# Two small tiles moved in front of the low weight tiles, so that the low weight tiles lie 64 bytes further within 512 bytes

## The chip, the cores and the metric

The kernel runs on one core of one Trainium2 chip. The metric is the time of one execution on the device in microseconds; a version's time is the median of its runs. One further execution was profiled, and all durations below come from that one.

## What is computed

Three transformer layers over one sequence of 256 tokens with 1024 features, in float32: an mLSTM layer and a short-convolution layer, each followed by a squared-ReLU MLP of width 4096, then a layer with retention and pooling, cross-attention to a memory of 256 tokens, and a gated MLP with a convolution. Nearly all of the arithmetic is the products of the activations with dense weight matrices:

```python
for i in range(DEPTH):                       # 2 layers
    h = rms_norm(x, g[0])
    h = mlstm_mixer(h, ...) if i % 2 == 0 else short_conv_mixer(h, ...)
    x = x + rms_norm(h, g[1])
    h = sqrelu_mlp(rms_norm(x, g[2]), w_mlp_up[i], w_mlp_down[i])
    x = x + rms_norm(h, g[3])
# then one layer more
h = rmsnorm(x, mix_norm_g)
x = x + concat([y_ret, y_pool]) @ w_out      # retention and pooling, from h @ w_in
x = x + cross_attn(rmsnorm(x, xa_norm_g), mem_n, xa_wq, xa_wkv, xa_wo)
x = x + conv_glu_ffn(rmsnorm(x, ffn_norm_g), ffn_w_up, ffn_conv_w, ffn_conv_b, ffn_w_down)
return rmsnorm(x, final_norm_g)
```

## The kernel before

**Tiles.** The activations lie transposed, features on the 128 partitions and the 256 tokens along a row, as 8 chunks (`x`, [128, 8, 256]). All weights come from memory as one sequence of slabs, in the order in which they are used. A slab is 1 MB, [128, 2048] float32: 8 blocks of the contraction by 256 output columns. The loads go to four tiles `raw0` to `raw3` in turn (line 366, SyncE).

**Splitting.** A product of two float32 numbers is made of three products of shorter ones. Each slab is split in halves of 1024 columns. ScalarE writes the high part, rounded to fp32r, into `wH` (line 790), and VectorE writes what is left, `raw - wH`, into `wL` (line 1230). There are two tiles of each, `wH0`, `wH1`, `wL0`, `wL1`, used in turn. The activations are split in the same way into `xnH` (line 804, ScalarE) and `xnL` (line 1237, VectorE), the memory into `memH` and `memL` (line 1244), the mixers' outputs into `mixH` and `mixL` (line 1272), the MLPs' hidden values into `hH` and `hL`.

**Products.** For each block of 128 by 128 weights TensorE runs three matmuls with 256 moving columns, each with a weight load of its own (lines 404 to 406):

```python
pe.matmul(psum[:, n, 0:T], wH[w][:, wc], aH[:, ac, :], start=start, stop=False)
pe.matmul(psum[:, n, 0:T], wH[w][:, wc], aL[:, ac, :], start=False, stop=False)
return pe.matmul(psum[:, n, 0:T], wL[w][:, wc], aH[:, ac, :], start=False, stop=stop)
```

In the phases that want tokens on the partitions (lines 431 to 433) the activations are the stationary operand, and `wH`, `wH`, `wL` the moving one. Other small products are put between the blocks of a slab by hand (`between`): sums of squares for the norms (line 472), scores, transposes.

**Order.** Every engine has its own written order and waits on semaphores. TensorE waits for the low half of the weights (`weights_ready`), and ScalarE, before it writes `wH` again, for the slab two before. VectorE and ScalarE also take the results out of the two PSUM tiles `po`. GpSimd adds squares for the norms (lines 1793 to 1800), computes the inverse roots (line 1806) and adds part of the residual (line 1817).

**Where the tiles lie.** SBUF is laid out by hand by `sb`, which hands out addresses within a partition one after the other, each size rounded up to 32 bytes:

```python
place = [nc.sbuf_base + (-nc.sbuf_base) % 64]
def sb(name, shape, dt, at=None):
    size = int(np.prod(shape[1:])) * 4
    if at is None:
        off = place[0]
        place[0] += (size + 31) // 32 * 32
```

The base is 16512, which is 128 past a multiple of 512. Each of `raw`, `wH`, `wL` and `x` takes 8192 bytes, a multiple of 512, so in the kernel before all of them begin 128 bytes past a multiple of 512, and so does `par`, the table of gains (1312 bytes). `warm` (4 bytes, written once at the start, line 854) and `ms` (8 bytes, the mean squares of a norm, line 1250) follow, 32 bytes each. `xnH`, `xnL`, `memH`, `memL`, `memk`, `memv`, `y`, `squares`, `mem`, `hH`, `hL`, `mixH` and `mixL` begin 64 bytes past a multiple of 512; `cgate` and `cval` of the last MLP 128 past it, `apad` 64 and 96 past it.

Of the kernel before, what the change touches and what calls it, by code (L numbers as in the profile page):

```python
# [9 lines left out]
P = 128  # L10
T = 256
TT = T // P
# [60 lines left out]
def build(nc, xT, memT, pos, weights, wgate, params, poolw, tri, mask, select, decay, freq, recount, out):  # L73
    f32, f32r, i32 = mybir.dt.float32, mybir.dt.float32r, mybir.dt.int32
# [3 lines left out]
    with ctx:  # L78
# [7 lines that stand above are left out]
            else:  # L86
                off = at[0]
                at[0] += (size + 31) // 32 * 32
            return nc.alloc_sbuf_tensor_at(name, list(shape), dt, offset=off)
# [4 lines left out]

        raw = [sb(f"raw{i}", [P, SLAB], f32) for i in range(RAW)]
        wH = [sb(f"wH{i}", [P, SLAB], f32r) for i in range(HL)]
        wL = [sb(f"wL{i}", [P, SLAB], f32r) for i in range(HL)]
        x = sb("x", [P, C, T], f32)
        par = sb("par", [P, NPAR], f32)
        warm = sb("warm", [P, 1], f32)  # L100
        ms = sb("ms", [P, TT], f32)
        minus_half = sb("minus_half", [P, 2 * NH], f32)
        rtok = sb("rtok", [P, TT], f32)
        rmem = sb("rmem", [P, TT], f32)
# [1896 lines left out]
```

## Time and profile before

| | |
|---|---|
| median of 3 runs | 995.93 us (992.37 to 1000.08) |
| the profiled execution's own time | 998.9 us |
| its span, first to last instruction | 996.5 us |
| mean granted TensorE clock | 0.994 of full speed |
| TensorE matmuls busy | 960.1 us, 96% |
| VectorE busy | 660.3 us, 66% |
| ScalarE busy | 534.8 us, 54% |
| GpSimd busy | 186.4 us, 19% |
| DMA | 49.5% of the 16 engines' time, 172 MB |

The profiled execution took 2.4 us more than its span. Matmuls are pipelined: a record of one lasts longer than the distance to the next, so several are in flight, and what an engine achieves is read from how many start in a stretch of time and not from the duration of one. Idle time stands with the engine that waited, together with what released it.

### The profile page before, as it was taken

What the parts mean: (1) busy time and instruction counts of PE and PEld (TensorE: products, weight loads), DVE (VectorE), ACT (ScalarE), POOL (GpSimd) and SP (SyncE); (2) the same over time, 40 slices, a digit from 0 to 9 for tenths busy, and PEclk for the clock granted to TensorE, in tenths of its full rate; (3) what the DMA queues carried; (4) which work ended last, traced back from release to release, by engine and by line L of the source; (5) the groups of instructions that cost most, each with busy time, mean ns of one, the idle gap of its engine ahead of it and who ended that gap; (6) DMA issues with size and microseconds to landing.
All of it is one profiled execution on the core that took longest, in us unless ns stands there. A gap on an engine that the chain in (4) does not pass through costs nothing.

```text
span 996.5 us, 20181 instructions
## 1 busy us (share of the span) xinstructions
PE 960.1 (96%) x8062; PEld 946.0 (95%) x8062; DVE 660.3 (66%) x843; ACT 534.8 (54%) x754; POOL 186.4 (19%) x159
## 2 busy tenths in 40 slices
PE   8999989999999899989999999889999999999995
PEld 7999989999999799989999999889999999999995
DVE  6667586665444877678665444774775779999642
ACT  5566646654444545556655443545554566666541
POOL 2121140000000400149100010455120122222101
PEclk9999999999999999999999999999999999999998
DMA  8533635555555355535655554544443545555521
GB/s 341 191 127 120 218 127 192 191 174 206 173 197 180 112 197 199 179 129 201 211 179 201 207 174 154 205 145 164 139 158 105 178 142 179 200 181 198 210 87 43
DMA packets 25844, 172.17 MB, mean 173 GB/s; under 512 B 3252, under 2 KB 3892, under 8 KB 5432
## 3 DMA queue, kind: packets, MB, share of 16 engines
q1 hardware_dynamic: 25784, 171.30, 49.5%
q8 instruction: 46, 0.75, 0.3%
q14 instruction: 14, 0.11, 0.0%
HBM read 170.24 MB, written 1.05 MB: 172 GB/s over the span
## 4 chain that ended last, share of the span: by engine, by line
PE 63%; DVE 15%; issue 6%; POOL 2%; ACT 2%; DVEq 1%; ACTq 0%; POOLq 0%
PE po L404 19%; PE po L405 19%; PE po L406 19%; DVE wL L1230 7%; DVE xnL L1237 2%; POOL rtok L1806 2%; DVE cval L1741 1%; DVE cgate L1741 1%; DVE apad L1728 1%; ACT wH L790 1%; PE po L432 1%; PE po L433 1%; PE po L431 1%; PE pn L479 1%; PE pc L728 1%
## 5 line engine op out<-in xcount | busy, mean ns | idle before, releaser
L1230 DVE TENSOR_TENSOR wL<-raw,wH 128x1024 fp32r<-128x1024 f32 x318 | 411.7, 1318 | 157.7 <-ACT wH L790 157.3
L790 ACT ACTIVATE wH<-raw 128x1024 fp32r<-128x1024 f32 x318 | 332.3, 1057 | 255.7 <-PE po L406 226.7
L404 PE MATMUL po<-xnH,wH 128*128 128x256 f32 x1376 | 391.4, 284 | 18.9 <-DVE xnL L1237 13.4
L405 PE MATMUL po<-xnL,wH 128*128 128x256 f32 x1376 | 383.6, 279 | 0.0
L406 PE MATMUL po<-xnH,wL 128*128 128x256 f32 x1376 | 383.4, 279 | 0.0
L404 PEld LDWEIGHTS po<-xnH,wH 128*128 128x128 f32 x1376 | 259.2, 188 | 24.3 <-DVE xnL L1237 10.3
L405 PEld LDWEIGHTS po<-xnL,wH 128*128 128x128 f32 x1376 | 260.5, 189 | 0.2
L406 PEld LDWEIGHTS po<-xnH,wL 128*128 128x128 f32 x1376 | 260.0, 189 | 0.0
L404 PE MATMUL po<-hH,wH 128*128 128x256 f32 x688 | 191.4, 278 | 1.3 <-DVE wL L1230 1.3
L405 PE MATMUL po<-hL,wH 128*128 128x256 f32 x688 | 191.3, 278 | 0.0
L406 PE MATMUL po<-hH,wL 128*128 128x256 f32 x688 | 191.3, 278 | 0.0
L1793 POOL TENSOR_TENSOR squares<-squares 128x512 f32<-128x512 f32 x26 | 39.7, 1526 | 515.9 <-ACT squares L838 362.1
L404 PEld LDWEIGHTS po<-hH,wH 128*128 128x128 f32 x688 | 129.1, 188 | 1.5 <-DVE wL L1230 1.5
L405 PEld LDWEIGHTS po<-hL,wH 128*128 128x128 f32 x688 | 130.2, 189 | 0.0
L406 PEld LDWEIGHTS po<-hH,wL 128*128 128x128 f32 x688 | 129.3, 188 | 0.0
L404 PE MATMUL po<-mixH,wH 128*128 128x256 f32 x256 | 71.8, 281 | 1.0 <-DVE mixL L1272 1.0
L405 PE MATMUL po<-mixL,wH 128*128 128x256 f32 x256 | 71.0, 277 | 0.0
L406 PE MATMUL po<-mixH,wL 128*128 128x256 f32 x256 | 71.0, 277 | 0.0
L1497 DVE SCALAR_TENSOR_TENSOR hrelu<-po,Rs 128x512 f32<-128x512 f32 x32 | 22.1, 691 | 49.2 <-PE po L406 49.0
L1237 DVE SCALAR_TENSOR_TENSOR xnL<-x,par,xnH 128x256 fp32r<-128x256 f32 x56 | 48.5, 918 | 7.4 <-ACT xnH L804 7.4
L404 PEld LDWEIGHTS po<-mixH,wH 128*128 128x128 f32 x256 | 48.1, 188 | 1.5 <-DVE mixL L1272 1.4
L405 PEld LDWEIGHTS po<-mixL,wH 128*128 128x128 f32 x256 | 48.3, 189 | 0.0
(284 smaller groups left out, 1083.8 us busy)
## 6 DMA issues: line engine op xcount, KB each, us to landing
raw<-in_weights SPq DMA_DIRECT2D x158, 1024.0 KB, 4.8
x<-in_xT SPq DMA_DIRECT2D x4, 256.0 KB, 5.7
raw<-in_weights SPq DMA_DIRECT2D x2, 512.0 KB, 5.5
mem<-in_memT SPq DMA_DIRECT2D x1, 1024.0 KB, 13.1
out<-y SPq DMA_DIRECT2D x4, 256.0 KB, 2.4
decayt<-in_decay SPq DMA_DIRECT2D x1, 512.0 KB, 3.7
poolwt<-in_poolw SPq DMA_DIRECT2D x1, 256.0 KB, 3.6
par<-in_params SPq DMA_DIRECT2D x1, 164.0 KB, 3.4
```

Source lines behind the costliest of these rows:

```text
L404: pe.matmul(psum[:, n, 0:T], wH[w][:, wc], aH[:, ac, :], start=start, stop=False)
L405: pe.matmul(psum[:, n, 0:T], wH[w][:, wc], aL[:, ac, :], start=False, stop=False)
L406: return pe.matmul(psum[:, n, 0:T], wL[w][:, wc], aH[:, ac, :], start=False, stop=stop)
L431: pe.matmul(psum[:, t, 0:256], aH[:, k, tc], wH[w][:, wc], start=k == 0, stop=False)
L432: pe.matmul(psum[:, t, 0:256], aL[:, k, tc], wH[w][:, wc], start=False, stop=False)
L790: act.activation(wH[b % HL][:, hs], raw[b % RAW][:, hs], ACT.Copy).then_inc(s_hi, 1)
L1230: dve.tensor_tensor(wL[b % HL][:, hs], raw[b % RAW][:, hs], wH[b % HL][:, hs].bitcast(f32), ALU.subtract)\
L1237: k = dve.scalar_tensor_tensor(xnL[:, c, :], x[:, c, :], col(gain, c), xnH[:, c, :].bitcast(f32), ALU.mult, ALU.subtract)
L1497: dve.scalar_tensor_tensor(hrelu[n % 2][:, :, :], slot(GROUP0[up] + n)[:, :, 0:T], 0.0, over_pair(Rs[:, :]), ALU.max, ALU.mult).then_inc(s ...
L1741: k = dve.scalar_tensor_tensor(c, apad[n % 2][:, e, tap:tap + T], w, c, ALU.mult, ALU.add)
L1793: pool.tensor_tensor(sq[0], sq[0], sq[p], ALU.add).then_inc(s_sqa, 1)
L1806: pool.tensor_tensor(r[:, :], ms[:, :], minus_half[:, 0:TT], ALU.pow).then_inc(s_r, 1)
```

## The change

Two declarations move up by a few lines. No instruction, wait, loop or transfer is added, removed or put elsewhere; each engine runs the same list of instructions in the same order, with other addresses in some operands.

```diff
         raw = [sb(f"raw{i}", [P, SLAB], f32) for i in range(RAW)]
         wH = [sb(f"wH{i}", [P, SLAB], f32r) for i in range(HL)]
+        warm = sb("warm", [P, 1], f32)
+        ms = sb("ms", [P, TT], f32)
         wL = [sb(f"wL{i}", [P, SLAB], f32r) for i in range(HL)]
         x = sb("x", [P, C, T], f32)
         par = sb("par", [P, NPAR], f32)
-        warm = sb("warm", [P, 1], f32)
-        ms = sb("ms", [P, TT], f32)
         minus_half = sb("minus_half", [P, 2 * NH], f32)
```

`warm` and `ms` take 32 bytes each. `wL0`, `wL1`, `x` and `par` therefore begin 64 bytes later, 192 past a multiple of 512. `warm` and `ms` now lie between `wH1` and `wL0`. `minus_half` and everything behind it, `xnH` and `xnL` among it, stay at their addresses, and so do `raw` and `wH`.

## Rows read from the trace of the kernel before

**Rows 1.** The page: busy us of each engine, and granted clock in 40 slices.

```profile
PE 960.1 (96%) x8062; PEld 946.0 (95%) x8062; DVE 660.3 (66%) x843; ACT 534.8 (54%) x754; POOL 186.4 (19%) x159
PEclk9999999999999999999999999999999999999998
```

**Rows 2.** Who waited for whom: us in total, times, longest us.

```profile
ACT wH L790 <- PE po L406: 226.7, 176, 4.4
DVE wL L1230 <- ACT wH L790: 157.3, 102, 6.2
...
PE po L404 <- DVE xnL L1237: 13.4, 11, 2.3
...
PE po L404 <- DVE wL L1230: 4.3, 5, 2.4
```

**Rows 3.** Stretches: us, busy (instructions) of PE, PEld, DVE, ACT, POOL; clock, DMA, GB/s.

```profile
160.00:320.00 160.00, 160.00 (x1361) 160.00 (x1360) 84.68 (x85) 79.08 (x92) 3.33 (x3) 1.00 0.55 186
455.00:600.00 145.00, 145.00 (x1281) 145.00 (x1281) 86.75 (x84) 80.07 (x97) 23.26 (x21) 1.00 0.56 192
880.00:930.00 50.00, 50.00 (x426) 50.00 (x426) 48.59 (x64) 30.31 (x43) 10.41 (x9) 1.00 0.55 189
```

**Rows 4.** Two of the weight loads' groups, 160 to 320 us: count | busy, mean ns.

```profile
L405 PEld LDWEIGHTS po<-xnL,wH 128*128 128x128 f32 x200 | 38.4, 192 | 0.0
L404 PEld LDWEIGHTS po<-xnH,wH 128*128 128x128 f32 x199 | 37.3, 188 | 0.0
```

**Rows 5.** Two of the groups of weight loads, 880 to 930 us.

```profile
L406 PEld LDWEIGHTS po<-xnH,wL 128*128 128x128 f32 x119 | 22.8, 192 | 0.0
L405 PEld LDWEIGHTS po<-xnL,wH 128*128 128x128 f32 x118 | 22.1, 188 | 0.0
```

**Rows 6.** Two of the groups of weight loads, 130 to 136 us.

```profile
L404 PEld LDWEIGHTS po<-memH,wH 128*128 128x128 f32 x15 | 2.9, 192 | 0.0
L406 PEld LDWEIGHTS po<-memH,wL 128*128 128x128 f32 x15 | 2.8, 188 | 0.0
```

**Rows 7.** Tile wL: duration ns min/median/max, first and last start us.

```profile
L406 PE MATMUL po<-xnH,wL x1376: 276/276/415, 9.6 to 921.6; 128*128 128x256 f32 x197
L1230 DVE TENSOR_TENSOR wL<-raw,wH x318: 1207/1221/2370, 7.7 to 974.1; 128x1024 fp32r<-128x1024 f32 x159
L433 PE MATMUL po<-wL,xnH x96: 276/279/281, 40.3 to 686.5; 128*128 128x256 f32 x96
```

**Rows 8.** Groups of the whole span: count | busy us, mean ns | idle before.

```profile
L406 PE MATMUL po<-xnH,wL 128*128 128x256 f32 x1376 | 383.4, 279 | 0.0
L406 PE MATMUL po<-hH,wL 128*128 128x256 f32 x688 | 191.3, 278 | 0.0
L406 PE MATMUL po<-mixH,wL 128*128 128x256 f32 x256 | 71.0, 277 | 0.0
```

**Rows 9.** VectorE's groups of lines 1237, 1244, 1266 and 1272, whole span.

```profile
L1237 DVE SCALAR_TENSOR_TENSOR xnL<-x,par,xnH 128x256 fp32r<-128x256 f32 x56 | 48.5, 918 | 7.4 <-ACT xnH L804 7.4
L1244 DVE SCALAR_TENSOR_TENSOR memL<-mem,par,memH 128x256 fp32r<-128x256 f32 x8 | 3.5, 474 | 0.0
L1266 DVE TENSOR_TENSOR sigo<-po,Rs 128x512 f32<-128x512 f32 x4 | 2.7, 687 | 0.8 <-PE po L406 0.8
L1272 DVE TENSOR_TENSOR mixL<-mixf,mixH 128x512 fp32r<-128x512 f32 x4 | 2.8, 689 | 1.1 <-ACT mixH L849 1.1
```

**Rows 10.** In order of time: start us, us; VectorE and GpSimd around line 1237.

```profile
132.14 0.89 DVE L1237 SCALAR_TENSOR_TENSOR xnL<-x,par,xnH 128x256 fp32r<-128x256 f32 x2 [1.16 <-ACT xnH L804]
...
630.16 5.95 DVE L1237 SCALAR_TENSOR_TENSOR xnL<-x,par,xnH 128x256 fp32r<-128x256 f32 x6
...
631.64 1.55 POOL L1793 TENSOR_TENSOR squares<-squares 128x512 f32<-128x512 f32 x1 [0.28 <-ACT squares L807]
...
634.22 1.61 POOL L1800 TENSOR_TENSOR squares<-squares 128x256 f32<-128x256 f32 x2
```

**Rows 11.** Duration of line 1741's groups, ns min/median/max.

```profile
L1741 DVE SCALAR_TENSOR_TENSOR cval<-apad,par,cval x44: 475/480/485, 815.7 to 929.4; 128x256 f32<-128x256 f32 x44
```

## The prediction, made before the changed kernel ran

> **What bounds the kernel now.** I read the page first, then who waited for whom, then the groups, and last single stretches of TensorE. TensorE has matmuls in flight for 96% of the span, and its clock is at the upper level (2.4 GHz) in every slice but a part of the last [rows 1]. ScalarE waits 226.7 us for TensorE, and VectorE waits 157.3 us for ScalarE, so the two splitting engines stand behind TensorE most of the time and not ahead of it. TensorE waits for the low weights only 4.3 us, in 5 waits, and 13.4 us for `xnL` behind a norm [rows 2]. So the end is set by how fast matmuls follow each other. A change of addresses can act in three ways: on that distance, on the duration of VectorE's, ScalarE's and GpSimd's operations, or on the transfers. I take them in turn.
>
> **How fast the matmuls follow each other.** The reader should count them. From 160 to 320 us, 1361 touch the stretch; two of these straddle its edges, so the distance is 160 us / 1359 = 117.7 ns. From 455 to 600 us it is 145 us / 1279 = 113.4 ns. Both stretches run at full clock with no idle time and the same work (an up projection, then the down projection) [rows 3]. So TensorE has two paces, 4.3 ns apart, and it keeps one for more than a hundred microseconds. This looks just like the trace of a bank conflict, and an address change might be aimed at it. The groups of weight loads tell what it is. At the slower pace one load in three takes 192 ns and the other two 188. In 160 to 320 us that is the load of line 405, from `wH` [rows 4]. In 880 to 930 us it is that of line 406, from `wL`, while the load of `wH` at line 405 has 188 [rows 5]. In 130 to 136 us it is that of line 404, again from `wH` [rows 6]. The addresses within 512 bytes are the same in all these stretches: weights at 128, activations at 64. A conflict between fixed addresses would sit on one of the three lines. This one sits on any of them, so it is a rhythm of the weight loads and matmuls with a period of three, that starts anywhere and then holds. Matmul durations go with it. In the phases by token, where the stationary operand is at 64 and the moving one at 128, the matmuls of line 433 also range between 276 and 281 ns [rows 7]: turning the distance of the two operands round did not remove either pace.
>
> **The change part by part.** It adds, removes and moves no instruction, and each queue and each wait stays. What is left is operands.
>
> *TensorE's reads of `wL`.* 2416 of its matmuls in the rows (1376 + 688 + 256 + 96) use `wL` [rows 7, 8], one in each triple. The 8 slabs that are multiplied with the memory add 8 x 16 = 128, which makes 2544 triples. What it costs: by the argument above, 0. What it could at most gain is the whole slow pace. I size that from mean durations, 276 ns at the fast pace and 281 at the slow one, the ends of line 433's durations. Line 406 with `xnH` has 383.4 us / 1376 = 278.6 ns, so 0.53 of those are at the slow pace; with `hH` 191.3 / 688 = 278.1, so 0.41; with `mixH` 71.0 / 256 = 277.3, so 0.27 [rows 7, 8]. Over these three that is (729 + 282 + 69) / 2320 = 0.47 of the triples. The same share of all 2544 triples is 1196 triples or 3588 matmuls; 3588 x 4.3 ns = 15.4 us. The other end: the 4044 at the fast pace all turn slow, 4044 x 4.3 ns = 17.4 us more. Two ends, -15 and +17 us, and I take 0, since the rows for no link to the address are direct.
>
> *VectorE's writes of `wL` (line 1230).* Today all three operands stand at 128. The median is 1221 ns for 1024 columns [rows 7]. Line 1272, all at one place too, needs 689 ns for 512 columns, and line 1266, which has one operand in PSUM, 687 [rows 9]. So two SBUF operands at the same place cost no more than one, and (1221 - 689) / 512 = 1.04 ns is the price of each further column, and that leaves no conflict to remove in line 1230. Tiles that differ by 64 already meet in `cval<-apad,cval` (apad at 64 or 96, cval at 128), with 475 to 485 ns for 256 columns [rows 11], against 474 for line 1244 with all tiles at 64 [rows 9]: nothing to lose either. I take 0. The ends: if line 1230 ran at no more than the columns' 1.04 ns, so 1065 ns, TensorE could gain what it waits for it, 4.3 us [rows 2]. The other end is the next point.
>
> *VectorE's reads of `x` (line 1237).* This is where the groups can mislead. `xnL<-x,xnH` takes 918 ns in the mean and `memL<-mem,memH`, the same operation on the same columns, 474 [rows 9]. `x` is at 128 and `xnH` at 64, while `mem` and `memH` are both at 64. Read as the price of lying 64 bytes apart, it would be 444 ns on 256 columns, and four times that on each half slab: 318 x 1.78 us = 565 us on VectorE, which would then be busy for 1225 us and bound the kernel. In order of time the cause is another one. The two at 132.14 us run in 0.89 us together, thus some 445 ns each, with the same addresses; between 132 and 133 us GpSimd has no row. The six from 630.16 us take 5.95 us, beside additions of GpSimd, one in 1.55 and two in 1.61 us among them [rows 10]. The stall belongs to GpSimd's work, and the change leaves that as it is.
>
> The Trainium skill, "SBUF — State Buffer", section "SBUF: two separate sides", says that engines contend only at a port pair that VectorE and GpSimd share, and that the loser is blocked for the whole instruction. By that rule the 918 ns are waits for GpSimd and the sum stays at 0; by the reading of addresses it would be +229 us. The trace agrees with the rule, by the 0.89 us for two.
>
> *The rest.* ScalarE's reads of `x` and GpSimd's additions into `x` are off the path, and ScalarE waits for TensorE anyway [rows 2]. `warm` is written once and `ms` 13 times with two elements. Transfers into `x` and `par` happen at the start, and `raw` keeps its place. I take 0 for all; a microsecond either way covers them.
>
> **The sum.** 998.9 us (the profiled execution) + 0 = 998.9 us. That execution lies 3.0 us above the median of the runs, and within the 7.7 us that they spread over. The forecast for a median is therefore the median before, 995.9, rounded to 996 us. A difference under 1% (10 us) can't be told from none with runs that spread so far. The spread itself may well be the share of the slow pace from run to run: 10 us would need 2300 of 7632 matmuls to change their pace.
>
> **The rivals.**
>
> *The slow pace goes (faster).* If the third load of each triple reads from another place than the first two, the rhythm of three may find no hold. For it: it has the same period as the sequence `wH`, `wH`, `wL`. Against it: the slow load was found on all three lines. It would give 995.9 - 15.4 = 980.5; from 880 to 930 us VectorE is nearly full, 48.59 of 50 us [rows 3], and would become the bound there, which keeps some 426 x 4.3 ns = 1.8 us. So 982 us.
>
> *The slow pace takes all (slower).* The place is the weight load of line 406, each time that TensorE turns from `wH` to `wL` and back. Until now the distance between the place of the weights and that of the activations never changes within a triple; with the change it does, and if that step itself costs what the slow load costs, each triple has its slow load and no stretch finds the fast pace. Price: 4.3 ns on each of the 4044 matmuls now fast, +17.4 us, 1013 us. It passes 1% when the slow share goes from 0.47 past 0.47 + 10 / (7632 x 0.0043) = 0.77. Against it: by token the distance is turned round, and the fast pace is there all the same [rows 7].
>
> *Tiles 64 bytes apart stall VectorE (much slower).* As worked out above, 1225 us. The 445 ns speak against it.
>
> *VectorE's split gets shorter.* 996 - 4.3 us, so 992 us: within 1%, even with as much again.
>
> *The change doesn't do what it says.* The shift might not be 64. 32 + 32 bytes are reserved for `warm` and `ms`, and nothing else moves ahead of `wL`, so I give it nothing of its own; the time would be 996 as well.
>
> **How the numbers follow.** No effect: 0.74. The slow pace goes, or goes for the most part: 0.12. The slow pace takes all, or most: 0.08. A shorter split: 0.05. VectorE stalls: 0.01. The predicted time is that of the likeliest case, 996 us. Its own range is 990 to 1002, from the runs before (992.4 to 1000.1) and a little on either side for a median of few runs. The range given goes toward the two rivals of pace without holding them whole: 984 to 1005. The chances: faster by over 1% 0.13 (the rival of pace, and a little of the case with the shorter split); slower by over 1% 0.09 (the two slower rivals); within 1% 0.78.
>
> **What would show it right or wrong.** Right: the matmuls still follow at 113.4 or 117.7 ns, both paces occur, perhaps in other stretches, and a slow load can be found on line 404 or 405, whose tile didn't move. Line 1230 keeps a median of 1221 ns, line 1237 its 0.45 us where GpSimd is idle, line 1272 its 689. TensorE's waits for lines 1230 and 1237 stay at some 4 and 13 us. The share of the slow pace may differ between two executions of one kernel; then a difference in one profile says nothing of the address. Wrong: a third pace, or no slow stretch at all, or slow loads only on line 406, or a median of line 1230 or 1237 that moved by more than a few ns.

## The result, and the profile after

The changed kernel takes 1016.76 us in the median of 4 runs (1015.28 to 1017.18). The kernel before has one run more than ahead of the change, and its median over the four is 998.0 us (992.37 to 1000.76). The ratio is 1.0192, with a 95% interval from 1.0146 to 1.0238: slower by nearly 2%. The profiled execution took 1016.92 us, its span is 1014.6 us against 996.5.

The page of the changed kernel, engines and clock first [rows 1], then the groups of the splits and of the matmuls with `xnH` and `xnL` [rows 8, 9]:

```profile
span 1014.6 us, 20181 instructions
...
PE 982.4 (97%) x8062; PEld 969.4 (96%) x8062; DVE 659.8 (65%) x843; ACT 536.8 (53%) x754; POOL 187.3 (18%) x159
...
PEclk9999999999999999999999999999999999999997
...
L1230 DVE TENSOR_TENSOR wL<-raw,wH 128x1024 fp32r<-128x1024 f32 x318 | 411.3, 1317 | 165.9 <-ACT wH L790 165.5
...
L404 PE MATMUL po<-xnH,wH 128*128 128x256 f32 x1376 | 397.0, 289 | 16.7 <-DVE xnL L1237 12.4
L405 PE MATMUL po<-xnL,wH 128*128 128x256 f32 x1376 | 388.8, 283 | 0.0
L406 PE MATMUL po<-xnH,wL 128*128 128x256 f32 x1376 | 386.1, 281 | 0.0
...
L1237 DVE SCALAR_TENSOR_TENSOR xnL<-x,par,xnH 128x256 fp32r<-128x256 f32 x56 | 48.5, 918 | 7.4 <-ACT xnH L804 7.4
```

The added time lies on TensorE: 982.4 us busy where it was 960.1, with the same 8062 matmuls. The mean granted clock is 0.991, where it was 0.994, and it is 1.00 in the stretch shown below for both kernels. VectorE's busy time, ScalarE's and GpSimd's moved by 2 us at most. Line 1237 has its 918 ns unchanged, though `x` now lies 128 bytes from `xnH` and not 64.

Who waited for whom, with the lines that answer to [rows 2]:

```profile
ACT wH L790 <- PE po L406: 254.8, 196, 4.4
DVE wL L1230 <- ACT wH L790: 165.5, 107, 6.2
...
PE po L404 <- DVE xnL L1237: 12.4, 11, 2.3
...
PE po L404 <- DVE wL L1230: 1.8, 1, 1.8
```

The two engines that split the weights wait longer than before, 254.8 us for 226.7 and 165.5 for 157.3, and TensorE waits for `wL` 1.8 us for 4.3. So the slower engine is TensorE itself. The stretch from 160 to 320 us shows how (columns as in [rows 3], without the other engines). First the view by stretch of the changed kernel, then its groups of matmuls with `xnH` and `xnL`, then the same groups of the kernel before:

```profile
160.00:320.00 160.00, 160.00 (x1356) 1.00 0.55 189
```

```profile
L404 PE MATMUL po<-xnH,wH 128*128 128x256 f32 x205 | 57.9, 283 | 0.0
L405 PE MATMUL po<-xnL,wH 128*128 128x256 f32 x205 | 57.7, 282 | 0.0
L406 PE MATMUL po<-xnH,wL 128*128 128x256 f32 x205 | 57.3, 280 | 0.0
```

```profile
L406 PE MATMUL po<-xnH,wL 128*128 128x256 f32 x201 | 56.5, 281 | 0.0
L404 PE MATMUL po<-xnH,wH 128*128 128x256 f32 x200 | 56.2, 281 | 0.0
L405 PE MATMUL po<-xnL,wH 128*128 128x256 f32 x200 | 56.2, 281 | 0.0
```

Matmuls follow each other at 160 us / 1354 = 118.2 ns, neither of the two old paces. And the three lines no longer have one duration: 283, 282 and 280 ns in place of 281 for all three in this stretch before. The tile `wL` now lies at 192 within 512 bytes as the allocator gives it, so the change did what it says.

In the whole trace of after no long stretch runs at 113.4 ns. I went through the starts of all matmuls, 30 at a time, and kept the groups in which all are of lines 404 to 406 and follow each other without a gap. In after the mean distance of every one of 185 such groups lies between 118.2 and 118.5 ns. In before 106 of 180 lie at 113.3 and the other 74 at 117.8.

### The profile page after: what moved, and what is told of

It reads as the page before. It is cut to its first block, busy times and chain, and to the rows that moved or that the text cites. A ratio compares the mean times of both kernels' runs of the same rounds, so it can differ in the third digit from the quotient of the medians.

```text
span 1014.6 us, 20181 instructions
## 1 busy us (share of the span) xinstructions
PE 982.4 (97%) x8062; PEld 969.4 (96%) x8062; DVE 659.8 (65%) x843; ACT 536.8 (53%) x754; POOL 187.3 (18%) x159
## 4 chain that ended last, share of the span: by engine, by line
PE 85%; DVE 7%; issue 3%; POOL 2%; ACT 2%; DMA 1%; DVEq 0%; SPq 0%; ACTq 0%; POOLq 0%
PE po L404 25%; PE po L405 25%; PE po L406 25%; DVE xnL L1237 2%; DVE wL L1230 2%; PE po L431 2%; POOL rtok L1806 2%; PE po L433 2%; PE po L432 2%; PE pn L479 1%; ACT wH L790 1%; PE pn L472 1%; PE pc L728 1%; DMA raw<-in_weights 1%; DVE diag L1256 0%
## 5 line engine op out<-in xcount | busy, mean ns | idle before, releaser
L1230 DVE TENSOR_TENSOR wL<-raw,wH 128x1024 fp32r<-128x1024 f32 x318 | 411.3, 1317 | 165.9 <-ACT wH L790 165.5
L790 ACT ACTIVATE wH<-raw 128x1024 fp32r<-128x1024 f32 x318 | 334.4, 1058 | 284.6 <-PE po L406 254.8
L404 PE MATMUL po<-xnH,wH 128*128 128x256 f32 x1376 | 397.0, 289 | 16.7 <-DVE xnL L1237 12.4
L405 PE MATMUL po<-xnL,wH 128*128 128x256 f32 x1376 | 388.8, 283 | 0.0
L404 PE MATMUL po<-hH,wH 128*128 128x256 f32 x688 | 194.4, 283 | 0.0
L405 PE MATMUL po<-hL,wH 128*128 128x256 f32 x688 | 193.7, 282 | 0.0
L406 PEld LDWEIGHTS po<-mixH,wL 128*128 128x128 f32 x256 | 48.4, 189 | 0.0
```

Of the source, the lines that this page charges most:

```text
L790: act.activation(wH[b % HL][:, hs], raw[b % RAW][:, hs], ACT.Copy).then_inc(s_hi, 1)
L1230: dve.tensor_tensor(wL[b % HL][:, hs], raw[b % RAW][:, hs], wH[b % HL][:, hs].bitcast(f32), ALU.subtract)\
```

## The experiments

In what follows the offset is the place of the weights less the place of the activations (`xnH`, `xnL`, `memH`, `memL`, `hH`, `hL`, `mixH`, `mixL`). Before it is 128 - 64 = 64 for `wH` and `wL`. In the changed kernel it is 64 for `wH` and 128 for `wL`. All kernels compute all of the reference; only addresses differ. Each was timed together with the kernel before on one chip, and its ratio is to those runs. The kernel before itself had medians from 995.1 to 1007.1 us in these jobs, so medians of two different jobs compare to about 1% only. The added lines of an edit are all shown; where a tile is moved, `...` stands for the lines up to where it was.

### Which tile, and which address

Both weight tiles moved, so that no step is left within a triple (e1):

```diff
+        warm = sb("warm", [P, 1], f32)
+        ms = sb("ms", [P, TT], f32)
         wH = [sb(f"wH{i}", [P, SLAB], f32r) for i in range(HL)]
         wL = [sb(f"wL{i}", [P, SLAB], f32r) for i in range(HL)]
...
-        warm = sb("warm", [P, 1], f32)
-        ms = sb("ms", [P, TT], f32)
```

> wH, wL, x and par all at 192; raw at 128, xnH at 64. Step theory (what costs is that the place of the weights changes against that of the activations within a triple): both paces of 113.4 and 117.7 ns return, 992 to 1001 us. Place theory (weights at 192 are read worse than at 128, whatever wH does): no stretch at 113.4 ns, 1013 to 1020 us. Theory of x (x or par at 192 is what costs): 1013 to 1018 us.

Measured: 1021.96 us (1020.96 to 1025.07), ratio 1.0237 [1.0167, 1.0307]. Its stretch, TensorE alone:

```profile
160.00:320.00 160.00, 160.00 (x1350) 1.00 0.54 189
```

That is 160 / 1348 = 118.7 ns, slower than the changed kernel, and over all three ranges that I had given. The step theory, which my slower rival was built on, said 992 to 1001 us and falls as it stands: here the place doesn't change from `wH` to `wL`, and TensorE is slower still. Whether such a step adds a part of its own where the two do differ is another question, and this run doesn't answer it.

`x` and `par` alone (e2), with `warm` and `ms` behind `wL`:

```diff
         wL = [sb(f"wL{i}", [P, SLAB], f32r) for i in range(HL)]
+        warm = sb("warm", [P, 1], f32)
+        ms = sb("ms", [P, TT], f32)
         x = sb("x", [P, C, T], f32)
         par = sb("par", [P, NPAR], f32)
-        warm = sb("warm", [P, 1], f32)
-        ms = sb("ms", [P, TT], f32)
```

> Only x and par 64 bytes on (192), wH and wL at 128. Step theory and place theory: as before, 992 to 1001 us, stretches at 113.4 ns. Theory of x: 1013 to 1018 us, none at 113.4 ns.

Measured: 1003.32 us (995.29 to 1007.61), ratio 1.0037 [1.0001, 1.0072]. The stretch:

```profile
160.00:320.00 160.00, 160.00 (x1414) 1.00 0.55 196
```

160 / 1412 = 113.3 ns: the fast pace, in a stretch in which before had the slow one [rows 3]. The median is 2 us over the range that I had given, but the kernel before had 999.1 us beside it. Moving `x` costs at most 0.7%, and nothing of TensorE's pace.

`wL` and `par`, with `x` kept at 128 (e3):

```diff
         wH = [sb(f"wH{i}", [P, SLAB], f32r) for i in range(HL)]
-        wL = [sb(f"wL{i}", [P, SLAB], f32r) for i in range(HL)]
         x = sb("x", [P, C, T], f32)
-        par = sb("par", [P, NPAR], f32)
         warm = sb("warm", [P, 1], f32)
         ms = sb("ms", [P, TT], f32)
+        wL = [sb(f"wL{i}", [P, SLAB], f32r) for i in range(HL)]
+        par = sb("par", [P, NPAR], f32)
```

> wL at 192, x at its 128 (x moved in front of wL), par at 192. Step theory and place theory: 1013 to 1018 us, mean distance 118.2 ns. Theory of x: 992 to 1001 us.

Measured: 1016.2 us (1015.15 to 1017.0), ratio 1.0166 [1.0098, 1.0234], the changed kernel's time. Its stretch has the changed kernel's 1356 matmuls too:

```profile
160.00:320.00 160.00, 160.00 (x1356) 1.00 0.54 190
```

`par` moved in e2 without a loss, so `wL` carries the whole loss.

`wL` moved by 512 bytes (e4): `ident`, a tile of 512 bytes, in front of it.

```diff
+        ident = sb("ident", [P, P], f32)
         wL = [sb(f"wL{i}", [P, SLAB], f32r) for i in range(HL)]
...
-        ident = sb("ident", [P, P], f32)
```

> wL 512 bytes on, at 128 again within 512 (ident moved in front of it); x and par 512 on too. If the place within 512 bytes counts: 992 to 1001 us, both paces. If any change of wL's address against wH counts: 1013 to 1018 us.

Measured: 994.45 us (992.34 to 1002.44), ratio 0.9962 [0.9919, 1.0004]. It is the place within 512 bytes that counts. These four leave one question: is 192 a bad place for weights, or is it the offset against the activations?

### Place or offset

Everything 64 bytes on (e5), by a gap in front of `raw`; and the weights in place with the activations 64, 320 and 128 bytes on (e6, e7, e8), by a gap in front of `xnH`:

```diff
+        sb("gap0", [P, 16], f32)
         raw = [sb(f"raw{i}", [P, SLAB], f32) for i in range(RAW)]
```

```diff
         rmem = sb("rmem", [P, TT], f32)
+        sb("gap1", [P, 16], f32)
         xnH = sb("xnH", [P, C, T], f32r)
```

(16 elements of gap1 in e6, 80 in e7, 32 in e8; the gaps are never written. Everything that is declared behind `xnH` moves along with it.)

> Everything 64 bytes on: weights at 192, activations at 128, their offset still 64. Offset theory (the pace depends on the offset of the weights against the activations within 512 bytes): as before, 992 to 1003 us, stretches at 113.4 ns. Place theory (weights at 192 are bad in themselves): 1016 to 1025 us, no stretch at 113.4 ns.

Measured: 1003.28 us (997.16 to 1008.36), ratio 1.002 [0.998, 1.006]. With weights at 192 the kernel is as fast as before, within the interval, as long as the activations move too. The place theory falls. Two stretches of e5, TensorE alone:

```profile
160.00:320.00 160.00, 160.00 (x1361) 1.00 0.53 187
455.00:600.00 145.00, 145.00 (x1234) 1.00 0.53 189
```

Here the stretch from 455 us has 145 / 1232 = 117.7 ns, where before had 113.4 [rows 3], and e2 had the fast one in the first stretch. So at offset 64 the same stretch has one pace in one kernel and the other in the next. How much of the trace is fast goes with the time of the profiled execution. Of the groups of 30 the fast ones are

| run | fast groups | its time, us |
|---|---|---|
| h1 (below) | 138 of 184 | 992.98 |
| e2 | 124 of 185 | 997.1 |
| before | 106 of 180 | 998.9 |
| e4 | 79 of 185 | 1002.44 |
| e5 | 44 of 184 | 1005.69 |

The order is the same in both columns. With 7152 matmuls on lines 404 to 406 and 4.4 ns for each, the ends of the table would lie some 16 us apart by my estimate; measured are 12.7. Only one execution of each kernel was profiled, so whether the share differs as much between executions of one kernel isn't shown.

> Activations 64 bytes on, weights in place: both at 128, offset 0. Offset theory with a cost that grows with the offset (64: 998 us, 128: 1021 us): at most 990 us, stretches below 113.4 ns or all at it. Offset theory with a collision where both streams begin at one place: over 1016 us. Place theory (only the weights' own place counts): 992 to 1003 us.

Measured: 1027.35 us (1026.75 to 1027.95), ratio 1.0288 [1.0216, 1.0361]. The stretch:

```profile
160.00:320.00 160.00, 160.00 (x1336) 1.00 0.52 185
```

160 / 1334 = 119.9 ns. With weights and activations at the same place TensorE is slowest. The weights' place is that of before, so this is the place theory's second refusal, and the theory of a cost that grows with the offset falls as well.

> Activations 320 bytes on (384), weights at 128, offset 256, as far apart as 512 bytes allow. Offset theory: a time that differs from before by over 1% on either side, and a pace other than 113.4 and 117.7 ns is possible. Place theory: 992 to 1003 us.

Measured: 1027.42 us (1026.08 to 1029.75), ratio 1.0295 [1.0221, 1.0369], and 1336 matmuls in the stretch. Offset 256 is the same as offset 0, to 0.1 us in the median.

> Activations 128 bytes on (192), weights at 128, offset -64. If only the size of the offset counts: 992 to 1003 us with both paces. If its sign counts too: another time, over 1% away. Place theory: 992 to 1003 us.

Measured: 1012.76 us (1009.72 to 1013.89), ratio 1.0136 [1.0062, 1.021]. The sign counts. The fast pace isn't quite gone at offset -64: 7 of 184 groups of 30 have 113.3 to 113.4 ns, the others 117.8.

### The offset in steps of 32 bytes

The same gap in front of `xnH`, with 8, 24, 40 and 56 elements (e9 to e12).

> Activations 32 bytes on (96), weights at 128, offset 32. Known so far: offset 64 gives 998 us, 0 and 256 both 1027, 128 gives 1022, -64 gives 1013, so the pattern repeats after 256 bytes. Smooth theory (the pace changes gradually with the offset): between 1000 and 1025 us. Steps of 64 bytes (only offsets in whole 64 bytes tell): like 0 or like 64, 1027 or 998 us.

> Activations 96 bytes on (160), offset -32, which is 224 within 256. Smooth theory: between offset 0 and -64, so 1013 to 1027 us. Steps of 64: 1027 or 1013.

> Activations 160 bytes on (224), offset -96, which is 160 within 256. Smooth theory: between offset 128 and -64, so 1013 to 1022 us. A better place than 64 would show as under 990 us.

> Activations 224 bytes on (288), offset -160, which is 96 within 256. Smooth theory: between offset 64 and 128, so 1000 to 1020 us; if the best offset lies between them, all stretches at 113.4 ns or less and under 988 us.

Measured, together with the offsets from above. The first distance is 160 us over the matmuls of the stretch from 160 to 320 us less two. The second is the mean over the whole trace, from one matmul of lines 404 to 406 to the next, with distances of 130 ns and more left out as gaps:

| offset within 256 | run | median us | ratio, 95% | stretch, ns | whole trace, ns |
|---|---|---|---|---|---|
| 0 | e6 | 1027.35 | 1.0288 [1.0216, 1.0361] | 119.9 | 119.9 |
| 32 | e9 | 1016.34 | 1.0152 [1.0099, 1.0205] | 118.3 | 118.3 |
| 64 | e5 | 1003.28 | 1.002 [0.998, 1.006] | 117.7 | 116.6, of 113.3 and 117.8 |
| 96 | e12 | 1017.47 | 1.0177 [1.0119, 1.0234] | 118.7 | 118.1 |
| 128 | e1 | 1021.96 | 1.0237 [1.0167, 1.0307] | 118.7 | 119.0 |
| 160 | e11 | 1026.44 | 1.0256 [1.0202, 1.031] | 119.9 | 119.9 |
| 192 | e8 | 1012.76 | 1.0136 [1.0062, 1.021] | 117.7 | 117.6 |
| 224 | e10 | 1009.77 | 1.0102 [1.0063, 1.014] | 116.6 | 116.9 |

The smooth theory held at 32 and 96 but not at 224 and 160. 224 is faster than both its neighbours, 160 slower than both. No offset beats 64.

The same traces hold a second reading of each offset. In the phases by token the activations are the stationary operand and the weights the moving one, so the stationary operand's place less the moving one's has the opposite sign there. Here is the mean distance over the whole trace, read as before, by that offset:

| stationary less moving | lines 404 to 406, ns | by token, ns |
|---|---|---|
| 0 | 119.9 (e6) | 119.6 (e6) |
| 32 | 118.3 (e9) | 118.3 (e10) |
| -32 | 116.9 (e10) | 116.9 (e9) |
| 96 | 118.1 (e12) | 117.9 (e11) |
| -96 | 119.9 (e11) | 119.7 (e12) |
| 128 | 119.0 (e1) | 118.7 (e1) |

Each row agrees within 0.4 ns, while a change of sign is worth 1.4 ns at 32 and 1.8 ns at 96. So what counts is the place of the stationary operand less that of the moving one, whichever of the two holds the weights.

### One load of three, or two

`wH` at 192 and `wL` at 128, the change the other way round (f16): `wL` first, then `warm`, `ms` and `wH`.

```diff
-        wH = [sb(f"wH{i}", [P, SLAB], f32r) for i in range(HL)]
         wL = [sb(f"wL{i}", [P, SLAB], f32r) for i in range(HL)]
+        warm = sb("warm", [P, 1], f32)
+        ms = sb("ms", [P, TT], f32)
+        wH = [sb(f"wH{i}", [P, SLAB], f32r) for i in range(HL)]
         x = sb("x", [P, C, T], f32)
         par = sb("par", [P, NPAR], f32)
-        warm = sb("warm", [P, 1], f32)
-        ms = sb("ms", [P, TT], f32)
```

> wH at 192 (offset 128), wL at 128 (offset 64), x at 192: the change the other way round. If every load outside offset 64 hinders the matmuls by itself, two loads of three do so, and the time lies between the changed kernel and both at 192: 1017 to 1022 us. If it is the step between wH and wL that costs: as the changed kernel, 1014 to 1018 us, below 1022. If only the loads of wL tell: 992 to 1003 us.

Measured: 1017.26 us (1015.67 to 1017.56), ratio 1.0134 [1.0037, 1.0231]. One load of three at offset 128 (the changed kernel) takes 1016.8 us, two of three 1017.3, all three (e1) 1022.0. The kernel before had 1007.1 us beside f16, more than in any other job, so the distances compare better than the medians: over the whole trace, read as above, they are 115.3 ns before, 118.2 in the changed kernel, 118.2 in f16 and 119.0 in e1. The number fits both expectations, so it doesn't decide between a step and a cost of each load. e1 shows that offset 128 costs without any step. Whether part of the loss in the changed kernel and in f16, where `wH` and `wL` do differ by 64 bytes, comes from the step stays open. Both runs do show that the cost isn't shared out evenly: one load of three at offset 128 costs 3.0 ns against before, two of three the same, all three 3.7.

### How narrow the good offset is

All weights in one tile, used from an inner place on, give offsets finer than 32 bytes:

```diff
-        wH = [sb(f"wH{i}", [P, SLAB], f32r) for i in range(HL)]
-        wL = [sb(f"wL{i}", [P, SLAB], f32r) for i in range(HL)]
+        wall = sb("wall", [P, 2 * HL * SLAB + 8], f32r)
+        wH = [wall[:, 4 + i * SLAB:4 + (i + 1) * SLAB] for i in range(HL)]
+        wL = [wall[:, 4 + (HL + i) * SLAB:4 + (HL + i + 1) * SLAB] for i in range(HL)]
```

This is g1; g3 begins 6 elements in. g2 and g4 begin 4 and 2 in, with `warm` ahead of `wall`.

> Weights at 144, activations at 96, offset 48. Known: offsets 32, 64, 96 give 1016, 998, 1017 us, each step of 32 its own time. If the good offset is a range, 48 lies in it: 992 to 1003 us or below. If it is one exact offset: about 1005 to 1016 us.

> Weights at 176, activations at 96, offset 80. Range theory: 992 to 1003 us or below. One exact offset: about 1005 to 1017 us.

> Weights at 152, activations at 96, offset 56. Range theory: as before or, if the best lies below 64, under 990 us with nearly all stretches at the fast pace. One exact offset: already over 1003 us.

> Weights at 168, activations at 96, offset 72. Range theory: as before or, if the best lies above 64, under 990 us with nearly all stretches at the fast pace. One exact offset: already over 1003 us.

Measured: offset 48 (g1) 1019.23 us, ratio 1.0221 [1.0135, 1.0307]; 80 (g2) 1021.82, 1.0237 [1.0152, 1.0322]; 56 (g3) 1015.05, 1.0171 [1.0086, 1.0255]; 72 (g4) 1017.29, 1.0195 [1.0111, 1.028]. The range theory falls for weights laid out like this, and 48 and 80 lie above even my range for one exact offset. Eight bytes off, two float32 columns, and nearly the whole loss of the changed kernel is there. The stretch at offset 56, TensorE alone:

```profile
160.00:320.00 160.00, 160.00 (x1360) 1.00 0.53 190
```

It has 160 / 1358 = 117.8 ns, which is as good as the slow pace of before. Over the whole trace no group of 30 lies under 117.3 ns. So at 56 the slow pace is nearly as it was, and what is gone is the fast one.

One rival is left here. In all four of these kernels the weights begin at a place that is no multiple of 32 bytes, as they do nowhere else, and no run has such weights at offset 64. It may be the weights' place against multiples of 32 bytes that costs, and not the offset of 56 or 72. A run with weights and activations both 8 bytes on would tell.

### 256 bytes between the two weight tiles

Offsets 0 and 256 agree, but at the slow end. At the good end (h1):

```diff
         wH = [sb(f"wH{i}", [P, SLAB], f32r) for i in range(HL)]
+        gapw = sb("gapw", [P, 64], f32)
         wL = [sb(f"wL{i}", [P, SLAB], f32r) for i in range(HL)]
```

> A gap of 256 bytes in front of wL: wH at 128, wL at 384, activations at 320, so the offsets are -192 for wH and 64 for wL within 512 bytes, and 64 for both within 256. If the pattern repeats after 256 bytes at the good offset too: 992 to 1006 us, stretches at 113.4 ns. If it takes 512 bytes there: 1010 us or more, none at 113.4 ns.

Measured: 996.33 us (992.45 to 1002.88), ratio 1.0013 [0.9978, 1.0049]. Its stretches, TensorE alone:

```profile
160.00:320.00 160.00, 160.00 (x1414) 1.00 0.55 195
455.00:600.00 145.00, 145.00 (x1282) 1.00 0.56 197
```

Both are at the fast pace, 160 / 1412 and 145 / 1280 = 113.3 ns. The pattern repeats after 256 bytes here too. `wH` and `wL` lie 256 bytes apart within 512, and nothing is lost, since both are at 64 within 256. It doesn't settle whether a step of 64 bytes within a triple costs, for within 256 bytes there is no step here.

## Why the prediction was wrong

**What bounds the kernel** was right: TensorE, by the distance of its matmuls. The loss showed there and nowhere else.

**The step that failed** is "a conflict between fixed addresses would sit on one of the three lines. This one sits on any of them, so it is a rhythm", and the 0 that I took from it for TensorE's reads of `wL`. The rows were read rightly and excluded less than I said. They exclude a conflict that belongs to one tile. What the runs show is a dependence on the offset between the weights and the activations, and in the kernel before that offset was 64 for all three lines alike. Such a dependence must look the same on all three lines. The view could not tell it from a rhythm without an address, since on these three lines it held no load at another offset. It takes both: a rhythm that holds for a stretch (the two paces at offset 64, in other stretches in e2 and e5), and an offset that decides whether the fast one is found at all, and in how much of the trace. With `wL` at offset 128 it isn't found, the matmuls follow at 118.2 ns, and the term that I had at 0 is 18.8 us.

**The second support failed too.** By token the stationary and moving operands are turned round, which makes the offset -64. I took the fast durations there as proof that the offset does not matter. The fast pace does exist at -64, but it is rare. Taking three distances in a row and calling them fast under 114.5 ns in the mean, 0.21 of those by token are fast in before and 0.57 of those on lines 404 to 406. e8 turns the signs round: by token, now at 64, 0.43 are fast, and on lines 404 to 406, now at -64, 0.05, and it takes 1012.76 us. So -64 is not as good as 64. That the pace occurs among the 480 matmuls by token, of 7632 in all, said nothing of how often, and nothing at all of offset 128.

**The size.** The slower rival had the right engine and nearly the right price. It put 17.4 us on the 4044 matmuls of the fast pace, for 1013 us; measured are 18.8 us between the medians. In its own terms: 4044 x (118.2 - 113.4) ns = 19.4 us, and 3588 x (118.2 - 117.7) ns = 1.8 us, together 21.2 us. The span grew by 18.1. TensorE's waits gave some back (2.5 us less for `wL`, 1.0 less for `xnL`), as it was later itself. That the rival's price came so near is in part luck: it had all matmuls go to the old slow pace of 117.7, with a slow load in each triple, and measured is a third pace. Its cause, the step between `wH` and `wL`, isn't needed, by e1, and whether it plays any part is open. Its chance of 0.08 was too low, and so was the range's upper end of 1005.

**What held.** VectorE's median for line 1230 is 1222 ns, after 1221 [rows 7]. Line 1237 keeps its 918 ns with `x` in another place, so the false reading of its mean as a price of address was rightly put aside. Moving `x` and `par` alone left the time within 0.7% (e2). The reading of line 1272 had a fault that cost nothing: it isn't "all at one place", since `mixf` lies 96 bytes past a multiple of 512 and `mixH` and `mixL` 64, as `sb` hands out the addresses. The fast rival, that the slow pace might go, found no support: no other offset tried came under the kernel before.

**What the signs said.** I had named "a third pace, or no slow stretch at all" as what would make it wrong. After has the third pace, 118.2 ns, and by that sign the prediction was wrong. Another sign, that line 1230 or 1237 moves by more than a few ns, didn't come.

## What to carry to other kernels

When matmuls follow each other without a gap, compare their distance between stretches that do the same work; two values under a full clock are a sign that something below the program's level is in play, and the tiles' addresses may be part of it, as they were here. Before taking an observation as proof that addresses don't matter, ask whether the trace holds any case with another relation between the two operands; if it holds none, the cost of a shift is open on both sides. In a kernel with a weight load for each matmul, write down where stationary and moving tiles lie within 256 bytes against each other, keep that offset when tiles are added in between, and try a few offsets. Here the offset of 64 bytes, stationary less moving, was worth 1 to 3% against the eleven others tried. For other shapes and types of matmul no run shows anything.

## What the runs showed of the hardware

- TensorE's pace, for float32r matmuls of 256 columns with a load of 128 by 128 for each, depends on the address of the stationary operand less that of the moving one, within a partition: ratios of 0.996 to 1.004 at 64 (e2, e4, e5, h1), 1.0102 at 224, 1.0136 at 192, and 1.0288 and 1.0295 at 0 and 256. By token, with the operands turned round, the distances are those of the opposite sign, within 0.4 ns (116.9 and 118.3 ns at -32 and 32). The pattern repeats after 256 bytes: 0 and 256 agree, and at the good end h1, with 256 bytes more between the weight tiles, has 996.33 us. A shift of all tiles by 64 bytes does nothing (e5, 1.002), nor does one of `wL` by 512 (e4, 0.9962).
- At 56 and 72 the kernel takes 1015.05 and 1017.29 us, so the good place looks narrow; that these weights begin off a multiple of 32 bytes is the rival that no run excludes.
- At offset 64 two paces are stable, 113.4 and 117.7 ns. Which one a stretch takes differs between kernels at that offset, and the more is fast, the shorter the profiled execution (138 of 184 groups with 992.98 us, 44 of 184 with 1005.69). The kernels at offset 64 spread by 10 to 12 us in 10 runs each (e2, e4, e5, h1), those at the other offsets by 1 to 6 us in 4 to 7. That the spread within one kernel comes from the paces fits, but was not tested by itself.
- The splits kept their durations. From before through e12 and f16 the median of VectorE's `wL<-raw,wH` stays between 1219 and 1222 ns, that of ScalarE's `wH<-raw` between 1060 and 1062, and that of `xnL<-x,par,xnH` between 948 and 952.
- Open: what in SBUF or TensorE makes the pattern. Two read streams that meet in the same part of memory would give a period and a dependence on the offset, but no run looked at this apart. How the loss is made up in a triple whose loads have different offsets (the changed kernel, f16), and whether the step between them has a part in it, is open too.
